# Delta rule in chunks: the chunk inverses by one substitution ahead of the recurrence, and the preparation between the input projection's tiles

## The reference

```python
g = cumsum(g)                                   # within a chunk
decay = where(lower, exp(g_i - g_j), 0)
lmat  = where(strict, (k*beta) @ k.T * decay, 0)
u, w  = solve(lmat + I, [v*beta, k*beta*exp(g)])          # unit lower triangular
qk    = where(lower, q @ k.T * decay, 0)
# from chunk to chunk, state s:
v_new = u - w @ s
o     = (q*exp(g)) @ s + qk @ v_new
s     = s*exp(g_last) + (k*exp(g_last - g)).T @ v_new
```

## Time and profile before

| | us |
|---|---|
| median of 3 runs | 1191.23 |
| lowest, highest | 1188.52, 1194.25 |
| the profiled execution | 1195.28 |
| its span | 1193.5 |
| mean granted TensorE clock | 0.952 of full |
| TensorE busy in it | 1091.2 (91%) |
| DVE, ACT, POOL busy | 574.6, 429.4, 151.8 |

### The profile page before, as it was taken

The page is one execution under the profiler, slowest core; times in us unless marked ns, Lnnn a source line. Parts: engine busy times, 40 slices in busy tenths (PEclk is TensorE's granted clock), DMA queues, the critical chain, the costliest instruction groups (busy, mean ns, idle before and its releaser), DMA issues.

```text
span 1193.5 us, 22298 instructions
## 1 busy us (share of the span) xinstructions
PE 1091.2 (91%) x9169; PEld 935.4 (78%) x9169; DVE 574.6 (48%) x1270; ACT 429.4 (36%) x863; POOL 151.8 (13%) x246
## 2 busy tenths in 40 slices
PE   3999999799998688788988897999999999999997
PEld 3998998587777454445555555999999999999997
DVE  5576463555556671782444444326334333424433
ACT  6435462344443124563333434235213313312322
POOL 1000005233332011003444420000000000000000
PEclk8999997599999799898999997999999999999999
DMA  7222201200000123004656623213323222222212
GB/s 246 82 71 71 75 1 40 97 22 2 2 2 6 36 85 127 1 1 160 222 198 216 239 81 103 74 37 124 107 71 106 71 102 76 96 82 86 92 36 76
DMA packets 24991, 102.15 MB, mean 86 GB/s; under 512 B 7743, under 2 KB 8559, under 8 KB 18418
## 3 DMA queue, kind: packets, MB, share of 16 engines
q1 hardware_dynamic: 15674, 62.96, 15.5%
q0 software_dynamic: 9216, 37.75, 9.0%
HBM read 96.49 MB, written 4.22 MB: 84 GB/s over the span
## 4 chain that ended last, share of the span: by engine, by line
PE 81%; DVE 10%; ACT 5%; issue 2%; POOL 1%; DMA 0%; ACTq 0%; SPq 0%; DVEq 0%
PE PS L533 16%; PE PS L535 16%; PE PS L534 16%; PE PS L919 4%; PE PS L954 3%; PE PS L930 2%; PE PS L808 1%; PE PS L937 1%; PE PS L641 1%; PE PS L657 1%; PE PS L631 1%; PE PS L708 1%; PE PS L664 1%; ACT AB L1230 1%; PE PS L650 1%
## 5 line engine op out<-in xcount | busy, mean ns | idle before, releaser
L533 PE MATMUL PS<-XH,WH 128*128 128x272 f32 (+1 forms) x992 | 290.6, 293 | 2.9 <-DVE XL L1433 1.5
L535 PE MATMUL PS<-XH,WL 128*128 128x272 f32 (+1 forms) x992 | 290.2, 293 | 0.0
L534 PE MATMUL PS<-XL,WH 128*128 128x272 f32 (+1 forms) x992 | 289.3, 292 | 0.0
L533 PEld LDWEIGHTS PS<-XH,WH 128*128 128x128 f32 x992 | 189.2, 191 | 6.2 <-DVE WL L1433 3.2
L534 PEld LDWEIGHTS PS<-XL,WH 128*128 128x128 f32 x992 | 189.2, 191 | 0.1
L535 PEld LDWEIGHTS PS<-XH,WL 128*128 128x128 f32 x992 | 189.0, 191 | 0.0
L1063 ACT ACTIVATE WH<-RAW 128x2048 fp32r<-128x2048 f32 x47 | 90.0, 1916 | 205.0 <-PE PS L535 203.3
L533 PE MATMUL PS<-NH,WH 128*128 128x272 f32 x512 | 149.1, 291 | 0.8 <-DVE WL L1433 0.8
L535 PE MATMUL PS<-NH,WL 128*128 128x272 f32 x512 | 147.6, 288 | 0.0
L534 PE MATMUL PS<-NL,WH 128*128 128x272 f32 x512 | 146.6, 286 | 0.0
L1433 DVE TENSOR_TENSOR WL<-RAW,WH 128x2048 fp32r<-128x2048 f32 x47 | 107.7, 2291 | 72.5 <-ACT WH L1063 72.5
(11 more groups left out here) (305 smaller groups left out, 1645.9 us busy)
## 6 DMA issues: line engine op xcount, KB each, us to landing
RAW<-in_w_stream SPq DMA_DIRECT2D x47, 1024.0 KB, 4.9
XN<-in_hin SPq DMA_DIRECT2D x4, 512.0 KB, 6.1
out_y_p<-YO SPq DMA_DIRECT2D x4, 512.0 KB, 2.7
WQ<-in_wq SPq DMA_DIRECT2D x1, 1536.0 KB, 6.7
CST<-in_big SPq DMA_DIRECT2D x1, 1404.5 KB, 13.6
SS<-in_sstate SPq DMA_DIRECT2D x1, 1024.0 KB, 5.8
out_ssm_s<-SS SPq DMA_DIRECT2D x4, 256.0 KB
CN<-in_cache,IDX POOLq DMA_INDIRECT x64, 5.9
```

The lines of the kernel that those rows point to most:

```text
L533: pe.matmul(PS[:, b, 0:n], wh, xh[:, k, c:c + n], start=(k == 0), stop=False)
L534: pe.matmul(PS[:, b, 0:n], wh, xl[:, k, c:c + n], start=False, stop=False)
L535: last = pe.matmul(PS[:, b, 0:n], wl, xh[:, k, c:c + n], start=False, stop=(k == DT - 1))
```

## The change

Tiles are done in another order (`TILES`): 16 and 17 (gates) come seventh and eighth, the weight chunks are loaded accordingly. Nearly all of the preparation moves between tiles: the queries' norms after the sixth tile, the keys' norms, gates, decays and the compact products later, each at a place that is written out. For the products of keys and queries the keys are laid out by POOL in groups of four chunks (KG, two buffers); KBD and QBD are laid out in groups of four chunks by ACT and POOL, the first two ahead of the recurrence and the others within it.

The inverses of all chunks are now computed at once, ahead of the recurrence. The compact matrices (128 rows by 16 columns per chunk) are turned by 16 transposes to 35 rows, one for each chunk, copied by ACT to BU and XU, and DVE solves them by a substitution of 14 steps with two instructions each. Sixteen transposes bring XU back, and four DVE instructions weight its columns (TICW for the decayed keys, TICV for the values). The masks lose m_upper, and the second spread (SCR) is gone.

In a chunk TensorE now computes the transposed keys (KX) and values (VX) three chunks ahead, the decayed keys WT = KX by TIW two chunks ahead, the solved values one ahead, into the bank in which the product of WT and the state is then added. DVE scales that sum to VNS, four products of 32 rows with KX give the state's update, ACT copies the sum to VNC for attention. The samples' chunks are written along the same lines, with the queries' reduction behind W2. The four transfers of a gather of cached pages count on one semaphore, and the banks of the first query products are exchanged.

```diff
+TILES = list(range(6)) + [16, 17] + list(range(6, 16)) + list(range(18, 22))
+CHUNKS = [TILES[2 * i] // 2 for i in range(N_IN)]
...
-                for (c, n), b in zip(HALVES, (4, 5) if m < 4 else (6, 7)):
+                pe.wait_ge(sem("qk_squared"), m + 1)
+                if m == 4:
+                    pe.wait_ge(sem("qk_root"), 1)
+                for (c, n), b in zip(HALVES, (4, 5)):
...
+            def spread_decays():
+                pe.wait_ge(sem("act_step"), ACT_STEP["egl_copied"])
...
+            def key_products(b):
+                if b == 0:
+                    pe.wait_ge(sem("qk_normed"), 8)
+                elif b == 2:
+                    pe.wait_ge(sem("compact"), 1)
+                for u in range(16 * b, min(16 * b + 16, NU)):
+                    if u % 4 == 0:
+                        pe.wait_ge(sem("kg_done"), u // 4 + 1)
+                    c = 2 * CH * (u % 16)
+                    for p in range(PAIRS):
+                        last = pe.matmul(PS[32 * p:32 * p + 32, (6, 7, 6)[b], c:c + 2 * CH], KG[u // 4 % 2][:, u % 4, p, :, :],
+                                         KQT[:, p:2 * PAIRS:PAIRS, CH * u:CH * u + CH], start=True, stop=True)
+                    if u % 4 == 3 or u == NU - 1:
+                        last.then_inc(sem("kg_used"), 1)
...
+            def chunk_transposes(x):
+                pe.wait_ge(sem("b_ready"), 1)
+                if x >= 2:
+                    pe.wait_ge(sem("xu_copied"), x - 1)
+                for s in range(4 * x, 4 * x + 4):
+                    last = pe.transpose(PS[0:NU, 6 + x % 2, P * (s % 4):P * (s % 4) + P], AB[:, 0, :, s], ident)
+                last.then_inc(sem("bu_t"), 1)
...
+            for i, m in enumerate(TILES):
+                if i % 2 == 0:
+                    pe.wait_ge(sem("w_split"), i // 2 + 1)
...
+                if i >= 2 and TILES[i - 2] < 8:
+                    head_sums(TILES[i - 2])
+                if 7 <= i < 11:
+                    spread_norm(i - 7)
+                elif i == 11:
+                    gates_to_columns()
+                    gates_to_decays()
+                elif i == 13:
+                    spread_decays()
+                    spread_norm(4)
+                elif i == 14:
+                    spread_norm(5)
+                    spread_norm(6)
+                elif i == 15:
+                    spread_norm(7)
+                elif i == 16:
+                    key_products(0)
+                    key_products(1)
+                elif i == 17:
+                    key_products(2)
+                    sum_squares("cq", 3)
+                elif i == 18:
+                    chunk_transposes(0)
+                    chunk_transposes(1)
+                    pe.wait_ge(sem("root"), ROOT["cq"])
+                    sum_squares("ckv", 2)
+                elif i == 19:
+                    chunk_transposes(2)
+                    chunk_transposes(3)
+                elif i == 20:
+                    conv_transposes(0)
+                    conv_transposes(1)
+                    pe.wait_ge(sem("root"), ROOT["ckv"])
+                    latent_transposes(0)
+                    latent_transposes(1)
+                elif i == 21:
+                    conv_transposes(2)
+                    for x in range(2, 5):
...
+            def keys_values(u):
+                pe.wait_ge(sem("kbd_done"), u // 4 + 1)
                 if u >= 1:
                     pe.wait_ge(sem("kv_copied"), u)
+                pe.transpose(PS[:, 0, 0:P], KBD[:, u, :, :, :].rearrange("p x y t -> p (x y t)"), ident)
+                for p in range(PAIRS):
+                    last = pe.matmul(PS[32 * p:32 * p + 32, 0, P:P + DK], VBD[:, p, u, :, :], cst("ident2"), start=True,
+                                     stop=True)
+                last.then_inc(sem("kv_mm"), 1)
...
+            def decayed_keys(u):
+                pe.wait_ge(sem("kv_copied"), u + 1)
+                pe.wait_ge(sem("tiw_done"), u + 1)
+                if u >= 1:
+                    pe.wait_ge(sem("wt_copied"), u)
+                pe.matmul(PS[:, 3, 0:P], KX[u % 4][:, :], TIW[u % 2][:, :], start=True, stop=True).then_inc(sem("wt_mm"), 1)
...
+            def solved_values(u):
+                pe.wait_ge(sem("tiv_done"), u + 1)
+                if u >= 1:
+                    pe.wait_ge(sem("vnc_done"), u)
+                last = pe.matmul(PS[:, 2, 0:DK], TIV[u % 2][:, :], VX[u % 4][:, :], start=True, stop=(u >= NUP))
+                if u >= NUP:
...
+            def off_state(u, bank, state, width, first):
+                pe.wait_ge(sem("wt_copied"), u + 1)
+                for p in range(PAIRS):
+                    last = pe.matmul(PS[32 * p:32 * p + 32, bank, 0:width], WT[u % 2][:, 32 * p:32 * p + 32], state(p),
+                                     start=first, stop=True)
...
+            def attend(u):
+                if u < NUP:
+                    pe.wait_ge(sem("os_done"), u + 1)
+                pe.wait_ge(sem("vnc_done"), u + 1)
+                pe.wait_ge(sem("atx_done"), u + 1)
+                pe.matmul(PS[:, 1, 256:256 + DK], ATX[u % 2][:, :], VNC[:, :], start=True, stop=True)\
+                  .then_inc(sem("a_mm"), 1)
...
+            pe.wait_ge(sem("inverted"), 1)
...
+            for x in range(2):
+                for t in range(8 * x, 8 * x + 8):
+                    last = pe.transpose(PS[:, 6 + x, NU * (t % 8):NU * (t % 8) + NU],
+                                        XU[:, t, :, :].rearrange("u h s -> u (h s)"), ident[0:NU, 0:NU])
...
+            for u in range(NUP):
+                pe.wait_ge(sem("st_done"), u + 1)
+                off_state(u, 2, lambda p: ST[:, p, :], DK, False).then_inc(sem("v_mm"), 1)
...
+                    pe.wait_ge(sem("or_done"), u)
+                query_state(u, 1, lambda p: ST[:, p, :], DK)
+                if u + 3 < NU:
+                    keys_values(u + 3)
+                pe.wait_ge(sem("vns_done"), u + 1)
                 for p in range(PAIRS):
                     rows = slice(32 * p, 32 * p + 32)
-                    pe.matmul(PS[rows, 3, 0:P], KBD[:, p, u, :, :], ident, start=True, stop=True)
-                    last = pe.matmul(PS[rows, 3, P:P + DK], VBD[:, p, u, :, :], cst("ident2"), start=True, stop=True)
-                last.then_inc(sem("kv_mm"), 1)
-            def c1(u, state, width):
...
-                  .then_inc(sem("s_mm"), 1)
-                c4(u)
-                s3(u + 1)
-                kv(u + 1)
-                s4(u + 1)
+                    last = pe.matmul(PS[:, 4 + p, 0:DK], KX[u % 4][rows, :], VNS[rows, :], start=True, stop=True)
+                last.then_inc(sem("s_mm"), 1)
+                attend(u)
+                decayed_keys(u + 2)
+                solved_values(u + 1)
...
+                if before < 8:
+                    head_squares(before)
+                if i == 6:
+                    head_roots(0)
+                elif i == 7:
+                    gates_start()
+                elif i == 8:
+                    gates_log()
+                elif i == 12:
+                    head_roots(1)
+                    rates()
+                elif i == 14:
+                    act.wait_ge(sem("dve_step"), DVE_STEP["decay_diff"])
+                    act.activation(AB[:, :, :, :], AB[:, :, :, :], ACT.Exp, scale=-1.0).then_inc(sem("act_step"), 1)
...
-                           ACT.Exp).then_inc(sem("act_step"), 1)
-            act.wait_ge(sem("tile_done"), 22)
-            for p in range(PAIRS):
-                act.wait_ge(sem("qk_normed"), p + 1)
+                    root("ckv", 2, KV)
+                    act.wait_ge(sem("kg_used"), 9)
+                    copy_chunks(0)
+                    copy_chunks(1)
...
+            def lay_keys(x):
...
+                last.then_inc(sem("kbd_done"), 1)
...
             for u in range(NUP):
-                copy_ab2(u + 1)
                 scale_qs(u)
-                copy_ab4(u + 1)
-                copy_b8(u + 1)
-                copy_kv(u + 1)
-            for step in (copy_ab2, copy_ab4, copy_b8, copy_kv):
-                step(NU - 1)
+                copy_values(u)
+                copy_wt(u + 2)
+                if u + 3 < NU:
+                    copy_kv(u + 3)
+                if u % 4 == 1 and u // 4 + 2 < 9:
+                    lay_keys(u // 4 + 2)
             act.wait_ge(sem("or_done"), NU)
...
+                if i == 7:
+                    invert_norms(0)
+                elif 8 <= i < 12:
+                    normalise_head(i - 8)
+                if i == 8:
+                    gates_abs()
+                    rotary_key()
+                elif i == 9:
+                    gates_sums()
+                elif i == 13:
+                    invert_norms(1)
+                    rate_products()
+                elif i == 14:
+                    decay_differences()
+                    normalise_head(4)
+                elif i == 15:
+                    normalise_head(5)
```

(66 more changed lines are left out.)

848 lines of the change are left out of this document (381 added, 467 removed).

## The result

The changed kernel takes **1184.87 us** (median of 9 runs, 1179.63 to 1186.36), the kernel before 1191.23 beside it (9 runs, 1188.00 to 1194.65): ratio 0.9936, 95% interval 0.9915 to 0.9957. That is 0.6% faster, little but outside the noise. The forecast was 1136, range 1108 to 1165. The profiled execution took 1185.79, its span is 1184.0, against 1195.3 and 1193.5.

A forecast was written before the change was run, and what follows sets the result against it. It took TensorE's queue as the bound, then ACT's loop in the new chunk. Profiled 1195.3 + 19 (preparation) - 71 (chunks) - 3 (samples) = 1140, and 1136 as the median lies 4.1 lower; range 1108 to 1165.

The forecast's parts named there:

- third rival: Recurrence: clock stays at 1.2 GHz once eight full-size products go; chunks 142 us, total 1210, chance 0.04.
- half of it: Recurrence: TensorE's clock at its lower level for part of the chunks; total about 1175, chance 0.05.
- The period at full clock: Recurrence: 2.37 us per chunk, from ACT's loop of 2.19 plus 0.17 for laying keys; 33 chunks 78 us.
- Chunk 0: Start of the recurrence: at 250.5 against 231.76, 19 us later; bounds 222 and 262.
- place 6: Sixth place in the tile order: TensorE's head_sums(4) waits for ACT's first roots, 4.2 us idle.
- places 8 to 10: Tile stage: DVE's queued work delays the normalisations that spread_norm waits for; TensorE loses about 3 us.
- place 13: Tile stage: spread_decays waits for EGL through DVE and ACT; TensorE idles 5.2 us.
- place 16: Tile stage: key products wait for POOL's layout of the keys, nine groups of 1.5 us; 7.6 us lost.
- place 19: Tile stage: chunk transposes wait for ACT's copies, behind cq_norm and a table load; 2 us.
- moved work: Tile stage: TensorE's own work moved between tiles (gates, decays, key products, transposes) costs 17.5 us.
- clock term of 10: Tile stage: half clock behind five stalls and the gates' eight-row products adds 10 us, 5 to 15.
- The samples: The two sample chunks: right-hand side gone, queries' mask and reduction behind W2; 3 us saved, 0 to 4.

The follow-up runs named there:

- e1_one: Changed kernel plus one unread full-size product of 128 columns in each of the 33 chunks; 1204.16 us.
- e7_stage: Changed kernel with the tile stage's TensorE waits taken away by reordering queues and sharing the keys' layout between GpSimd and ScalarE, recurrence untouched; 1158.55 us.
- e2_three: Changed kernel plus three unread full-size products of 128 columns in each chunk; 1187.71 us.
- e4_full: Changed kernel with the state update's four 32-row products made one product of 128 rows by 256 columns again; 1156.80 us.
- e3_burst: Changed kernel plus 15 unread full-size products of 256 columns where TensorE waits ahead of the recurrence, none inside it; 1177.87 us.
- e9_move: e3_burst with the four page index instructions moved out of chunk 4 to behind the sample chunks; 1165.23 us.
- e13_gain: Changed kernel with stage waits removed, full-size state product, page indices behind the chunks, nine added products before them, GpSimd's gain multiply split into four chunks; 1118.14 us.

## Why the prediction was wrong, point by point

**The clock in the chunks** is the step that failed: +36.3 us (114.3 against 78). It stood as the third rival with 0.04, and half of it with 0.05. The argument against it was that TensorE would still be busy some 85% of the time. The runs show that busy time is not what counts: 100% busy stayed at 0.50 in the changed kernel, in e1_one and e7_stage, and in all three the eight full-size doubling products, of which I had written that they "keep it at 1.00", were gone. e2_three and e4_full show that full-size products in a chunk bring the clock back; no run takes the eight alone out of the kernel before. The mechanism was in the prediction, the chance given to it was wrong. Its price was wrong too, towards the dear side: the rival doubled the full-clock queue of 1.97 to 3.9 and added latencies for a period of 4.3 and 1210 us. Measured at half clock are 3.47 with no latency on top. With that period and the measured start the rival's own sum gives 1191 + 26 - 35 = 1182, 3 us under the measured time.

**The period at full clock** was right: 2.37 forecast, 2.31 to 2.49 in e3_burst and e9_move, a mean of 2.35. Part of that is luck: the sum was 2.19 and 0.17 for laying keys; measured are 2.31 and, 0.18 in every fourth chunk, 0.04. The four 32-row products, 0.35 within 0.13 to 0.80: at half clock TensorE goes on 0.64 us after their start (301.16 to 301.80), so by half of it 0.32. What I expected as its sign, idle time released by VNC, is there as 0.21 us a chunk released by ScalarE's copy of VX, a neighbour in the same queue.

**Chunk 0**: +26.1 instead of +19, inside the bound of 262 at 257.88. The waits, forecast and measured: place 6, 4.2 and 4.4; places 8 to 10, 3 and 2.7; place 13, 5.2 and 3.4; place 16, 7.6 and 9.0; place 19, 2 and 0.7. Sum 22 and 20.2, and e7_stage shows that they were the cause. Place 16 was dearer since GpSimd needs 1.8 us a group, not 1.5. The 2 us more that I had set beside it by the Trainium skill, "GPSIMD Engine Reference", section 8, had no test there: the low halves (186.13 to 188.42) lay ahead of the layout. The substitution, forecast 15.7, took 15.2 us on VectorE, from the first to the last of its 28 instructions:

```profile
236.69 0.35 DVE L1713 TENSOR_TENSOR MU<-BU,XU 35x112 f32<-35x112 f32 x1 [2.43 <-ACT XU L1205]
...
251.65 0.27 DVE L1715 TENSOR_TENSOR XU<-XU,MU 35x112 f32<-35x112 f32 x1
```

The tail behind tile 21 was 10.9 (its copy at 246.99 to 257.88), forecast 9. What was short is the clock and the moved work: 193.0 - 1.0 + 20.2 + 10.9 leaves 34.8 for both against 17.5 + 10. The moved work was not measured by itself. e7_stage gave back 10 us beside its waits, so the clock term of 10 was too small; with its bound of 15 most of the gap closes.

**The samples**: 3 us forecast, 0 measured. The removal was real: e13_gain takes 16.5. The change also moves GpSimd's gain multiply from ahead of the chunks to behind them, where it runs beside the one VectorE instruction of the samples' path that reads two tiles of SBUF. That move was in the diff and not in my steps; it cost 2.6 us (3.09 against 0.48). The clock took a share too: over the sample chunks it was 0.68 against 0.83 before, and the two groups of state products took 3.78 and 3.59 us against 3.24 and 3.40. For place 16 I had cited the Trainium skill, "GPSIMD Engine Reference", section 8, on instructions with two SBUF inputs; the same rule bore on this place, and here the trace agrees with it.

**The base**: I took the median as 4.1 below the profiled execution, as before; for the changed kernel it is 0.9 below. That is 3 us of the miss. Sum: 36.3 + 7.1 + 3.2 + 3.2 less 0.9 from the query projection on is 48.9, the difference of 1184.9 and 1136.

**Which case came**: none of mine in full. The stage came out as forecast, the recurrence as rival 3 at a lower price. The range ended at 1165 and left out rival 3 and its half, which had 0.09 together. The case "clock below 1.00 in the chunks" was named as what would make the prediction wrong, and it did.

## What to carry to other kernels

When a change takes full-size products out of a stage and leaves narrow ones, price the stage at both levels of TensorE's clock, and do not argue from busy time alone: here a queue full of narrow products ran at half clock for 114 us, and putting one full-size product back, with more work in it, gained 28 us. Look for the longest stop of TensorE ahead of and inside such a stage, since here the chunks began at 1.00 only in the kernels that filled it; a stop can cost its length and then the half clock behind it. And list every instruction that a diff moves, also the small ones that seem free (four index instructions, one gain): name what each stands ahead of in its queue, and what it runs beside.
